# Pairs of attention units in TensorE's queue, on one core of Trainium2

## The reference, cut to what matters

```
    o_cmp = ...                                   # compressed blocks, an earlier stage
    o_slc = lax.map(one_block, (..., qs, ids))    # softmax over the chosen key blocks
    o_win = banded_attention(q, kw, vw, C_WINDOW, slopes)   # causal window of 512 keys
    return gates[..., 0:1] * o_cmp + gates[..., 1:2] * o_slc + gates[..., 2:3] * o_win
```

## Time and profile before

| | |
|---|---|
| median of 3 runs | 772.91 us (769.65 to 776.05) |
| the profiled execution | 773.16 us |
| its span, first to last instruction | 771.2 us |
| mean granted clock of TensorE | 0.991 |
| the last attention stage | about 476 to 668 us of the span |

### The profile page before, as it was taken

How to read it: one execution, slowest core, us unless ns; L and a number is a source line. 1 busy time by engine, 2 the same in 40 slices (tenths; PEclk the granted TensorE clock), 3 DMA queues, 4 the chain that set the end, 5 groups by cost and what they waited for, 6 DMA issues and landing times.

```text
span 771.2 us, 15596 instructions
## 1 busy us (share of the span) xinstructions
PE 720.3 (93%) x5916; PEld 618.2 (80%) x5916; DVE 537.7 (70%) x1263; ACT 437.2 (57%) x1102; POOL 188.3 (24%) x118
## 2 busy tenths in 40 slices
PE   4999999999999999889988998989999999899996
PEld 4999878687778777668876787878999999788885
DVE  4796222044888888967778896999999999934232
ACT  5774122013566556667746563879999999722211
POOL 2674000000000000000143332516276552122120
PEclk9999999999999999999999998999999999999998
DMA  8620548165135621153144322300003101143331
GB/s 324 210 81 25 196 134 231 51 186 166 55 91 135 167 82 56 55 132 102 57 127 126 110 68 87 84 2 3 2 3 110 57 2 57 68 151 120 127 110 54
DMA packets 34090, 77.12 MB, mean 100 GB/s; under 512 B 5472, under 2 KB 14048, under 8 KB 33376
## 3 DMA queue, kind: packets, MB, share of 16 engines
q1 hardware_dynamic: 34016, 76.13, 32.6%
HBM read 57.77 MB, written 18.35 MB: 99 GB/s over the span
## 4 chain that ended last, share of the span: by engine, by line
PE 51%; DVE 19%; ACT 14%; issue 9%; DMA 4%; POOL 1%; SPq 1%; ACTq 0%; DVEq 0%; POOLq 0%
ACT n_probs L1787 5%; DVE n_probs L1850 4%; ACT n_probsT_high L1797 4%; PE o_acc L2228 3%; PE o_acc L2226 3%; PE o_acc L2227 3%; PE a_projected L199 3%; PE nat L823 3%; PE a_projected L200 3%; PE a_projected L201 3%; DMA w_raw<-in_w_feat 3%; PE features L809 2%; PE features L811 2%; PE features L810 2%; DVE branches_b_c L1092 2%
## 5 line engine op out<-in xcount | busy, mean ns | idle before, releaser
L1787 ACT ACTIVATE n_probs<-n_probs,n_negated_max 128x640 f32<-128x640 f32 (+7 forms) x128 | 94.9, 741 | 19.1 <-DVE n_negated_max L1850 18.1
L1859 DVE SCALAR_TENSOR_TENSOR n_probsT_low<-n_turned,n_probsT_high 128x512 f16<-128x512 f32 (+3 forms) x192 | 94.3, 520 | 14.1 <-ACT n_probsT_high L1797 11.9
L183 POOL TENSOR_TENSOR w_and_keys_low<-w_raw,w_and_keys_high 128x1024 fp32r<-128x1024 f32 x6 | 14.4, 2394 | 289.6 <-ACT w_and_keys_high L168 289.3
L865 PE MATMUL n_turned<-identity,n_probs 128*128 128x128 f32 x528 | 80.8, 277 | 3.9 <-ACT n_probs L1787 3.1
L1797 ACT ACTIVATE n_probsT_high<-n_turned 128x512 f16<-128x512 f32 (+3 forms) x192 | 81.1, 458 | 2.9 <-PE n_turned L865 2.3
L1998 PE MATMUL n_scores<-w_and_keys_high,stacks 128*128 128x256 f32 (+2 forms) x192 | 74.7, 389 | 3.8 <-DVE n_negated_max L1850 3.7
L865 PEld LDWEIGHTS n_turned<-identity,n_probs 128*128 128x128 f32 x528 | 60.8, 142 | 12.7 <-ACT n_probs L1787 9.5
L1999 PE MATMUL n_scores<-w_and_keys_low,stacks 128*128 128x256 f32 (+2 forms) x192 | 62.0, 333 | 0.0
L199 PE MATMUL a_projected<-xT_high,w_and_keys_high 128*128 128x512 f32 x144 | 57.3, 398 | 0.9 <-ACT staged L208 0.7
L200 PE MATMUL a_projected<-xT_low,w_and_keys_high 128*128 128x512 f32 x144 | 56.4, 392 | 0.0
L201 PE MATMUL a_projected<-xT_high,w_and_keys_low 128*128 128x512 f32 x144 | 56.3, 391 | 0.0
(11 more groups left out here) (288 smaller groups left out, 2126.9 us busy)
## 6 DMA issues: line engine op xcount, KB each, us to landing
w_raw<-in_w_feat SPq DMA_DIRECT2D x23, 512.0 KB, 4.0
weights_then_b_and_s_raw<-features SPq DMA_DIRECT2D x30, 256.0 KB, 4.7
stacks<-a_parts SPq DMA_DIRECT2D x48, 128.0 KB, 4.1
features<-staged SPq DMA_DIRECT2D x22, 256.0 KB, 4.3
branches_b_c<-in_x SPq DMA_DIRECT2D x8, 512.0 KB, 4.3
silu_gates<-staged SPq DMA_DIRECT2D x16, 256.0 KB, 2.2
gatesT<-silu_gates SPq DMA_DIRECT2D x8, 512.0 KB, 5.2
keys_and_w_out_raw<-in_w_out SPq DMA_DIRECT2D x4, 1024.0 KB, 4.9
```

What stands on the lines that cost most here:

```text
L865: mm = nc.tensor.transpose(dst[:, j, :], src[:, c:c + P], ident[:, :])
L1787: nc.scalar.activation(pr[:, n % PS, 0:w], pr[:, n % PS, 0:w], ACT.Exp, scale=-1.0, bias=nmax[:, hb % 4, qt:qt + 1], accum_out=sums[:, hb ...
L1859: nc.vector.scalar_tensor_tensor(out=ptl[:, g % GS, 0:k, :], in0=tp[g % TS][:, 0:k, :], scalar=PSCALE, in1=pth[:, g % GS, 0:k, :], op0=ALU ...
```

## The change

The unit loops of the three engines are written by pairs w, w+1. TensorE's queue becomes S(w+2), S(w+3), T(w), T(w+1), V(w-2), V(w-1). ScalarE's becomes E(0), E(1), then H(n), E(n+2) for each n, with the copy at the end of the pair. VectorE's loop is rewritten, too, and issues B(n+2), L(n) for each n as before. No buffer, no size and no instruction is added or removed.

```diff
@@ scalar
             exponentials(0)
-            for n in range(UN):
-                if n + 1 < UN:
-                    exponentials(n + 1)
-                high_part(n)
-                if n % NT == 2 and n > NT:
-                    bring_out(n // NT - 1)
+            exponentials(1)
+            for wide in range(0, UN, 2):
+                for n in (wide, wide + 1):
+                    high_part(n)
+                    if n + AHEAD < UN:
+                        exponentials(n + AHEAD)
+                if wide % NT == 2 and wide > NT:
+                    bring_out(wide // NT - 1)
@@ vector
-            for n in range(UN):
-                if n + AHEAD < UN:
-                    add_bias(n + AHEAD)
-                low_part(n)
+            for wide in range(0, UN, 2):
+                pair = (wide, wide + 1)
+                for n in pair:
+                    if n + AHEAD < UN:
+                        add_bias(n + AHEAD)
+                    low_part(n)
...
@@ tensor
-            for n in range(UN):
-                if n + AHEAD < UN:
-                    scores(n + AHEAD)
-                turn(n)
-                if n >= 2:
-                    values(n - 2)
+            for wide in range(0, UN, 2):
+                pair = (wide, wide + 1)
+                for n in pair:
+                    if n + AHEAD < UN:
+                        scores(n + AHEAD)
+                for n in pair:
+                    turn(n)
+                for n in pair:
+                    if n >= 2:
+                        values(n - 2)
```

More of the change, by code:

```diff
@@ L1884, in _ @@
             ch.link(nc.vector.tensor_scalar(small[:, 2:3], small[:, 0:1], 0.5 * (1.0 - LAM_INIT), None, ALU.mult))
-            for n in range(UN):
-                if n + AHEAD < UN:
-                    add_bias(n + AHEAD)
-                low_part(n)
[L1889 to L1894, removed]
+            for wide in range(0, UN, 2):
[4 more added lines that the diff above has]
+                    low_part(n)
+                    if n in SUMS_AT:
+                        a_sums(SUMS_AT.index(n))
+                    if n == RSTD_AT:
+                        a_rstd()
+                    if n % NT == 1 and n > NT:
+                        invert_sums(n // NT - 1)
             invert_sums(LAST)
```

## The result

The changed kernel takes 788.68 us (median of 4, 786.64 to 791.74) against 772.82 (median of 4 runs, one more than above) for the kernel before: ratio 1.0215, 95% interval 1.0181 to 1.0250, which is 14.0 to 19.3 us. It is slower by 15.9 us. The forecast was 788.7, from a sum of +15.8.

A forecast was written before the change was run, and what follows sets the result against it. It took alternating ScalarE and VectorE waits as the bound, TensorE off the chain. Loop 14.3, copies 1 and sums of squares 0.5 gave +15.8 us on the profiled 773.16, 789.0; less 0.25 to the median, 788.7; range 775 to 798.

The forecast's parts named there:

- The bound and the question: Last attention stage: waits ran over ScalarE and VectorE, without TensorE; asked whether the new order puts TensorE on that chain.
- The loop's links: Turn, high part, low part, row minimum, score, next turn close in one pair: fixed 1.42 us, 25.0 a head.
- VectorE ... fits L(w+1) and B(w+4) into it: VectorE's work between a row minimum and the next pair's low part: at the tightest about 1.5 us into 1.65.
- TensorE's own work: Turns, values and scores in the attention stage: 22.2 us a head; the fullest pair ties with the loop at 2.97.
- rival 2: Faster, 765 us: back-to-back turns feed ScalarE earlier, switches go; floor is TensorE's 22.2 us a head; chance 0.07.
- The copies: ScalarE's 15 output copies at their new place: 0.05 us uncovered each, between nothing and 0.47; 1 us in all.
- The sums of squares: VectorE's two sums of squares in the first two heads stand inside the loop: 0.5 us, between 0 and 2.4.
- rival 4: TensorE stops in almost every pair, so the clock could fall through the stage: +160 us; chance 0.01.
- No change: 773 us, 770 to 779: ScalarE and VectorE taking turns stays longest, scores find their bank free; chance 0.12.
- Slower by more: 798 to 806 us: loop and old chain add up, output copies cost their full 0.47 us each; chance 0.07.
- The rule on the fullest engine: Improve the fullest engine first: TensorE's weight loads, 21.29 of 23.16 us, would promise 0.6 us a head, about 5 us.
- the main term: Attention stage: 1.84 us more a head, 0.23 a pair, over 62 of 64 pairs: 14.3 us.

The follow-up runs named there:

- experiment 1: Changed kernel with the scores taken apart again and the values still paired: 773.06 us, ratio 1.0029 to the kernel before.
- experiment 2: Changed kernel with only the scores paired, turns and values alternating as before the change: 789.32 us, ratio 1.0238 to the kernel before.
- Experiment 12: Changed kernel with ScalarE's 15 output copies back at their old place: 794.27 us, ratio 1.0289 to the kernel before.
- Experiment 9: Changed kernel with one repeated one-tile low part per pair on VectorE, beside the loop: 790.31 us, ratio 1.0250 to the kernel before.
- experiment 11: Changed kernel with VectorE and ScalarE also ordered by pairs, so all three engines are: 770.58 us, ratio 0.9986 to the kernel before.
- experiment 3: Changed kernel with VectorE by pairs too, two row minima and then two low parts: 771.55 us, ratio 1.0017 to the kernel before.
- experiment 4: Changed kernel with VectorE by pairs and TensorE's order of the kernel before: 787.00 us, ratio 1.0204 to the kernel before.

## Why the prediction was right, point by point

**The bound and the question.** Right: before, the chain ran over ScalarE and VectorE, and the change put TensorE on it. Experiments 1 and 2 show it is the scores' place: with the scores apart again 0.18 of the 2.1 us a head remain, and with the scores alone paired the loss is whole.

**The loop's links.** Right to 0.02 us each, see the timeline above. The signs came, too: over the stage TensorE's idle time at scores is 21.2 us (about 20 forecast), and 61 weight loads of scores waited for a row minimum (50 to 60 forecast). By pairs of a head, predicted and measured (distance between turns, from 596.02 to 621.28 us):

| pair, tiles | predicted | measured |
|---|---|---|
| window 5+1 | 3.26 | 3.27 |
| full 8+4 | 3.41 | 3.43 |
| full 7+3 | 3.13 | 3.27 |
| full 6+2 | 3.10 | 3.11 |
| full 5+1 | 3.26 | 3.27 |
| window 5+4 | 3.01 | 3.02 |
| window 5+3 | 2.87 | 2.90 |
| window 5+2 | 2.97 | 2.99 |

**The one pair that is off.** "VectorE ... fits L(w+1) and B(w+4) into it" failed in full 7+3. I had left out the reciprocal of the row sums, 0.11 us, that stands there, too, and VectorE's wait for H(w+1), 0.24 us:

```profile
602.24 0.08 DVE L1852 DVE_READ_ACCUMULATOR2_ANT n_negated_max<- 128x1 f32 x1
602.56 0.69 DVE L1861 SCALAR_TENSOR_TENSOR n_probsT_low<-n_turned,n_probsT_high 128x512 f16<-128x512 f32 x1 [0.23 <-ACT n_probsT_high L1797]
603.17 0.19 DVE L1868 RECIPROCAL n_sums<-n_sums 128x8 f32<-128x8 f32 x1
603.28 0.91 DVE L1852 CUSTOM_DVE_ANT_0 n_probs<-n_scores,n_bias_chosen 128x768 f32<-128x768 f32 x1
604.11 1.15 DVE L1861 SCALAR_TENSOR_TENSOR n_probsT_low<-n_turned,n_probsT_high 128x512 f16<-128x512 f32 x2
```

The wait 0.24, L(w+1) 0.61, the reciprocal 0.11 and B of 6 tiles 0.83 us are 1.79 us from the end of B(w+3) to L(w+2), and 1.65 was there. It costs 0.14 us of the 0.25 by which the head was under-forecast (25.0 against 25.26), 2 us in the whole.

**TensorE's own work.** Counted wrong, without harm to the forecast. A head has 66 tiles to turn and to multiply (528 turns in 8 heads), not 68, so by the prediction's own costs its work is 21.9 us and not 22.2, and rival 2's floor lies that much lower. Nor is the pair with the scores of 8 + 4 tiles the fullest: full 7+3, with 10 tiles turned, 12 multiplied and 7 scored, comes to 3.10 us. The loop's 3.13 was still above it, and the measured 3.27 is above both. The upper bound has a slip as well: 1.42 + 0.05 + 2 x 0.03 is 1.53 and not 1.51, a head of 25.9 us and 794.

**The copies.** I had put +1 us (15 times 0.05 is 0.75) for what they leave uncovered at their new place. The pairs that begin behind a copy, full 6+2 and window 5+2, are 0.01 and 0.02 us over their links, so the term should have been nothing. Experiment 12 adds what the prediction didn't ask: at their old place in this loop the copies would have cost 0.44 us a head, so the change's own ScalarE edit saved it from being some 3.4 us slower still.

**The sums of squares.** Right in size: the head that holds them went from 24.85 to 27.25 us, 0.3 us more than a head without them; I had 0.5.

**The small steps behind L(24).** Missed: the sum has no term for them. The head that holds them was 2.93 us over its neighbours and is now 4.36 over. They, too, stand in the loop, and TensorE stopped for 3.31 us behind them. Then came rival 4 on a small scale: the granted clock, the third number from the end in the second fence, fell from 1.00 to 0.50 (2.4 to 1.2 GHz) for 3.4 us, and ten turns took 2.33 us where ten take 1.25 at full clock:

```profile
525.44 0.58 PE L2002 MATMUL n_scores<-w_and_keys_high,stacks 128*128 128x256 f32 x1 [3.31 <-DVE n_negated_max L1852]
...
526.03 2.33 PE L865 MATMUL n_turned<-identity,n_probs 128*128 128x128 f32 x10
```

```profile
522.00:524.00 2.00, 0.13 (x2) 0.00 (x0) 1.69 (x10) 0.59 (x3) 0.00 (x0) 1.00 0.00 0
524.00:526.00 2.00, 0.56 (x2) 0.56 (x3) 1.71 (x7) 0.58 (x2) 1.33 (x1) 0.72 0.01 4
526.00:528.00 2.00, 2.00 (x12) 2.00 (x11) 1.17 (x4) 0.97 (x4) 2.00 (x1) 0.50 0.03 8
```

That is 1.1 of the 1.4 us, and other work in that stretch was slower, too. Experiment 9 has the same steps at the same place. There TensorE stopped for 2.99 us, the clock stayed at 1.00, and that head was 2.52 us over its neighbours, not more than in the kernel before:

```profile
523.45 0.39 PE L2006 MATMUL n_scores<-w_and_keys_high,stacks 128*128 128x256 f32 x1 [2.99 <-DVE n_negated_max L1853]
523.67 0.28 PE L2007 MATMUL n_scores<-w_and_keys_low,stacks 128*128 128x256 f32 x1
523.79 1.25 PE L865 MATMUL n_turned<-identity,n_probs 128*128 128x128 f32 x10
```

So the 1.4 us look like the clock's, by one execution of each; that the steps stand in the loop cost little by itself. The length of one stop didn't decide it: in experiment 11 the clock fell, at 519.5 us, behind one of 2.06 us. In the steady heads of the changed kernel, where weight loads of scores wait up to 0.8 us in most pairs, the clock stayed at 1.00, as I had it. The Trainium skill, TensorE: Matmul & The Clock Gate, HAM oscillation — how this bites in real kernels, tells of a clock that falls during long waits, and the 3.31 us agree with it; its section A second HAM failure mode tells of a clock that swings with short idle times, and the steady heads don't show that.

**The rivals.** No change and faster are out by the measured ratio and by experiments 1 to 4. Slower by more is out as a whole; a piece of it, the clock, is the point above. The rule on the fullest engine (Trainium skill, Perfetto Trace Analysis, Identifying the Most-Contended Engine) was weighed with TensorE's share alone. Taken over all engines of the earlier trace rows it names ScalarE, 21.84 us busy against 21.29 of weight loads and 21.39 of VectorE, and so promises nothing for fewer switches on TensorE. What fewer switches are worth shows experiment 11, where nothing of the loop is left and the switches are saved: a head is 23.04 us against 23.16, 0.12 us instead of the 0.6 that I priced, and not to be told from none in the time.

**The sum.** Terms: steady heads, forecast 14.3, in the profile (25.26 - 23.16) / 8 x 62 = 16.3 us; copies +1, measured nothing; sums +0.5, measured 0.3; small steps 0, measured 1.4, mostly the clock. That makes 18.0 of the 18.6 us by which the profiled executions differ (spans of 771.2 and 789.8), while the medians differ by 15.9. The executions of one kernel vary by 5 us and the interval of the ratio is as wide, so the forecast's agreement to 0.1 us is luck: the main term was 2 us short, and +1 us for copies stood in for part of it. The head's length is what the theory was tested on, 0.25 us short of 2.1.

**Open.** What holds a head at 23.0 to 23.3 us in four different orders (before, 1, 3, 11). TensorE's own work is 21.9 us by the prediction's costs, ScalarE is busy 21.6 in experiment 11. The waits that remain there are short and of several kinds, and no experiment took one away alone.

## What to carry to other kernels

When two engines pass work back and forth, write down for each wait the steps that stand ahead of it in each queue, follow them until they close, and count how many units the loop spans: reordering one queue can shorten that span, from three units to two here, without touching any duration, and an engine's idle time doesn't cover what stands in such a loop. Here two queues had to be grouped alike or neither: one alone cost 2 us a head, both together nothing and gained nothing. The links of the loop can be read beforehand from places where the receiver already waits, and here they summed to within 1% of a head. Rare long stops of TensorE are worth a look of their own: here a steady loop of short ones left the clock at 1.00, and one of 3.31 us went with 3.4 us at half of it.

## What the runs showed of the hardware that wasn't expected

A VectorE addition with both operands in SBUF (256 columns) took 0.41 to 0.42 us in the 81 cases of experiments 6 and 7 in which no GpSimd instruction was running at its start. In the other 47 it ended 0.28 to 0.34 us behind the GpSimd instruction, all of them elementwise operations on SBUF tensors, and so took up to 3.83 us (606.76 + 3.83 = 610.59 against 605.77 + 4.54 = 610.31). The low part and the row minimum, which have one operand in PSUM, kept their durations to within 0.02 us inside the same kind of GpSimd instruction. 64 such additions cost 56 us inside the loop and 27 beside it over the changed kernel's 788.68, the falls of the clock included; 64 times 0.41 would be 26.
